# Two transformer blocks on one core: 512-column down products, head sums in parts of the array, refilled gaps and a reworked first stage

## The reference, cut to what matters

```python
x = first_block(x, c, ...)      # 256 tokens, width 2048
#   mod = silu(c) @ w_ada + b_ada -> sh1, sc1, g1, sh2, sc2, g2
#   h = rms_norm(x, mix_norm_pre) * (1 + sc1) + sh1
#   three mixers on h @ w_in, gated and merged, @ w_o
#   x = x + g1 * rms_norm(merged @ w_o, mix_norm_post)
#   h = rms_norm(x, mlp_norm_pre) * (1 + sc2) + sh2
#   y = square(relu(h @ w_up)) @ w_down           # 2048 -> 8192 -> 2048
#   x = x + g2 * rms_norm(y, mlp_norm_post)
return second_block(x, c_2, ctx_2, ...)
#   the same frame; mLSTM and differential attention over 256 tokens of x
#   and 256 of a context; then conv_ffn, 2048 -> 2 * 5632 -> 2048
```

## Time and profile before

| what | us |
|---|---|
| median of 3 runs | 3325.54 (3325.36 to 3334.14) |
| the profiled execution | 3323.51 |
| its span in the trace | 3321.3 |
| TensorE busy with matmuls | 3223.8 (97%) |
| VectorE busy | 2260.6 (68%) |
| ScalarE busy | 1332.6 (40%) |

### The profile page before, as it was taken

How to read it: one execution, slowest core, us unless ns; L and a number is a source line. 1 busy time by engine, 2 the same in 40 slices (tenths; PEclk the granted TensorE clock), 3 DMA queues, 4 the chain that set the end, 5 groups by cost and what they waited for, 6 DMA issues and landing times.

```text
span 3321.3 us, 59467 instructions
## 1 busy us (share of the span) xinstructions
PE 3223.8 (97%) x26148; PEld 3119.3 (94%) x26148; DVE 2260.6 (68%) x2625; ACT 1332.6 (40%) x1455; POOL 1.7 (0%) x10
## 2 busy tenths in 40 slices
PE   7899999999999999999998999999998999999998
PEld 6899999999998999999998898989888999999998
DVE  2499765688876778898856756644756666666664
ACT  2343344434444433333454224422455444343444
POOL 0000000000000000000000000000000000000000
PEclk9999999999999999999999999999999999999999
DMA  9864443488893877777744763354333475655643
GB/s 356 335 209 163 153 153 136 175 330 330 313 347 141 311 286 264 261 253 279 274 164 153 304 239 144 127 211 161 115 139 121 173 253 190 216 209 194 237 165 122
DMA packets 106429, 722.87 MB, mean 218 GB/s; under 512 B 11676, under 2 KB 15388, under 8 KB 27196
## 3 DMA queue, kind: packets, MB, share of 16 engines
q1 hardware_dynamic: 100368, 703.64, 57.4%
q10 hardware_dynamic: 5804, 15.43, 1.5%
HBM read 712.40 MB, written 6.55 MB: 216 GB/s over the span
## 4 chain that ended last, share of the span: by engine, by line
PE 92%; DVE 3%; DMA 2%; ACT 1%; issue 1%; ACTq 0%; DVEq 0%
PE gemm L1006 52%; PE gemm L1015 26%; PE mix L1094 2%; DMA sb_raw<-stream 2%; PE mix L1006 1%; PE mix L1193 1%; PE gemm L1129 1%; PE mix L1457 1%; ACT sb_parts L516 1%; DMA sb_arena<-x_t 1%; DVE sb_arena L1722 1%; DVE sb_parts L1676 1%; PE mix L1015 1%; PE gemm L1530 0%; PE gemm L1523 0%
## 5 line engine op out<-in xcount | busy, mean ns | idle before, releaser
L516 ACT ACTIVATE sb_parts<-sb_raw 128x2048 fp32r<-128x2048 f32 (+2 forms) x499 | 913.7, 1834 | 1668.0 <-PE gemm L1015 1412.3
L1676 DVE TENSOR_TENSOR sb_parts<-sb_raw,sb_parts 128x2048 fp32r<-128x2048 f32 (+2 forms) x499 | 1089.9, 2186 | 401.6 <-ACT sb_parts L516 220.3
L1006 PE MATMUL gemm<-op_h,sb_parts 128*128 128x256 f32 x7232 | 898.5, 282 | 0.5 <-DVE sb_arena L1783 0.5
L1006 PEld LDWEIGHTS gemm<-op_h,sb_parts 128*128 128x128 f32 x7232 | 874.6, 188 | 1.5 <-issue 0.9
L1015 PE MATMUL gemm<-op_h,sb_parts 128*128 128x256 f32 x3616 | 466.3, 282 | 0.0
L1006 PE MATMUL gemm<-op_up,sb_parts 128*128 128x256 f32 x3456 | 438.5, 283 | 11.4 <-DVE op_up L2245 11.4
L1015 PEld LDWEIGHTS gemm<-op_h,sb_parts 128*128 128x128 f32 x3616 | 445.3, 188 | 0.0
L1006 PEld LDWEIGHTS gemm<-op_up,sb_parts 128*128 128x128 f32 x3456 | 422.7, 189 | 13.7 <-DVE op_up L2245 12.2
L1015 PE MATMUL gemm<-op_up,sb_parts 128*128 128x256 f32 x1728 | 228.2, 283 | 0.0
L1657 DVE CUSTOM_DVE_ANT_0 sb_raw<-sb_raw,sb_arena,sb_vec 128x2048 f32<-128x2048 f32 x96 | 224.2, 2348 | 1.1
L1015 PEld LDWEIGHTS gemm<-op_up,sb_parts 128*128 128x128 f32 x1728 | 216.2, 190 | 0.0
(11 more groups left out here) (339 smaller groups left out, 3302.6 us busy)
## 6 DMA issues: line engine op xcount, KB each, us to landing
sb_raw<-stream SPq DMA_DIRECT2D x611, 1024.0 KB, 5.0
sb_raw<-stream SPq DMA_DIRECT2D x64, 704.0 KB, 4.4
sb_raw<-stream SPq DMA_DIRECT2D x16, 768.0 KB, 7.6
sb_arena<-c_rows ACTq DMA_DIRECT2D x3, 1024.0 KB, 8.4
bias_rows<-sb_arena ACTq DMA_DIRECT2D x1, 2304.0 KB
sb_arena<-x_t ACTq DMA_DIRECT2D x4, 512.0 KB, 17.8
sb_arena<-ctx_t SPq DMA_DIRECT2D x1, 2048.0 KB, 10.7
x_keep<-sb_arena ACTq DMA_DIRECT2D x1, 2048.0 KB, 6.2
```

Source lines behind the costliest of these rows:

```text
L516: act.activation(parts[:, b % 2, 0, 0:kt, :], raw[:, slot, 0:kt, :], ACT.Copy).then_inc(hi_ready, 1)
L1006: ins = pe.matmul(out, l, r, start=(opens and i == 0 and x is xh), stop=False, skip_group_check=True)
L1676: dve.tensor_tensor(parts[:, b % 2, 1, 0:kt, :], raw[:, slot, 0:kt, :], parts[:, b % 2, 0, 0:kt, :].bitcast(F32), ALU.subtract).then_inc(t ...
```

## The change

1. `down_round` and `gemm_parts` replace `plain_round` and `gemm_T` in all down sections. The 32 high-weight matmuls of 256 columns become 16 of 512, whose moving operand is high and low half of `op_up` together; the two halves of the bank are added by VectorE (`add_halves`), or, in the first section, copied by ScalarE and added by VectorE (`first_round`).
2. `head_row` puts the 8 sums into four 32-column parts of the array, `spread_rows` spreads from four 32-row parts. VectorE now waits for all four banks at once.
3. In the three gaps the second block's splits move behind the root (ScalarE) and behind `residual` (VectorE). `gemm_two` takes 16 of its 32 low matmuls between the high ones. `norm_x` has 20 small matmuls of ones before it and 10 behind (`keep_warm`). In the middle gap there is no `norm_x`: the second block's `m_k` comes first, and the context's half of its first two blocks is multiplied there, with the norm of x between.
4. First stage: slots grow from 4 to 8 for the first 48 blocks. TensorE handles the shift's A block only; the scale's is stored like the later ones and reduced on VectorE (`scale_column`), by a row of silu(c) made at the start with four matmuls and four activations.

```diff
+            def gemm_parts(b, op, it=0, kt=KT, waits={}):
...
+                for k in range(kt):
...
+                    pe.matmul(out, parts[:, b % 2, 0, k, :], op[:, :, k, :], start=(k == 0), stop=False, skip_group_check=True)
+                pe.wait_ge(taken[slot], uses + 1)
+                for k in range(kt):
+                    ins = pe.matmul(bank(b)[:, 0:S], parts[:, b % 2, 1, k, :], op[:, 0, k, :], start=False, stop=(k == kt - 1),
...
+            def add_halves(acc, b):
+
+                step(dve.tensor_tensor(acc, bank(b)[:, 0:S], acc, ALU.add))
+                dve.tensor_tensor(acc, bank(b)[:, S:512], acc, ALU.add).then_inc(bank_read[BANK[b]], 1)
```

```diff
+                return pe.matmul(M[0][32 * g:32 * g + 32, 0:S], head_sum[:, 31 - j:63 - j], src, start=(j == 0), stop=(j == 1))
...
+                for j in range(2):
+                    for g in range(4):
+                        q = slice(32 * g, 32 * g + 32)
+                        ins = pe.matmul(M[g][:, j * S:(j + 1) * S], ident[q, 32 * g + j:32 * g + j + 1].to_broadcast([32, P]), rows[q, :],
...
+            def keep_warm(n):
...
+                for _ in range(n):
+                    pe.matmul(M[3][:, 0:P], ones[:, :], ones[:, :], start=True, stop=True)
...
+                        if k < KT // 2:
+                            with_low(i, k)
```

```diff
+EARLY_SLOTS, N_EARLY = 8, 48
...
-    + [("m_q", "G" * 8), ("m_k", "GAA" * 8), ("m_g", "G"), ("m_v", "GAA" * 8), ("m_o", "G" * 8),
+    + [("m_k", "GG" + "GAA" * 6), ("m_q", "GGA" * 4), ("m_g", "G"), ("m_v", "GAA" * 8), ("m_o", "G" * 8),
...
+                else:
+                    for c in range(4):
+                        context_part(1, range(4 * c, 4 * c + 4), 0, (0, 1))
+                        norm_part(sqx, *CHUNKS[c + 1])
...
+            def scale_column(r):
...
+                dve.wait_ge(loaded[slot], 16 * (uses + 1))
+                dve.tensor_tensor_reduce(w, w, c1_early, 1.0, v("b_ada", KT + r), ALU.mult, ALU.add, mod1[:, KT + r:KT + r + 1])\
+                   .then_inc(taken[slot], 1)
+                dve.wait_ge(taken[slot], uses + 1)
```

More of the change, by code:

```diff
@@ L763, in _ @@
                     silu_c(cctx_row, 3)
-                    rounds("down1_0", plain_round("down1_0", down1))
+                    rounds("down1_0", first_round("down1_0", down1))
                 elif q < 3:
@@ L968, in _ @@
                 if q == 0:
-                    rounds("down2_0", plain_round("down2_0", down2))
+                    rounds("down2_0", first_round("down2_0", down2))
                 elif q < 3:
@@ L1035, in features_wide, with gemm_two, with_low @@
                 product(b, [(out, True, [(lambda w, x, k=k: (w[:, k, :], x), opW[:, :, 0, k, :], opW[:, :, 1, k, :]) for k in range(KT)])])
-            def gemm_two(b, op, n):
+            def gemm_two(b, op, n, at=0):
+                def with_low(i, k):
+                    return pe.matmul(bank(b + i)[:, at:at + S], parts[:, (b + i) % 2, 1, k, :], op[:, 0, k, :], start=False,
+                                     stop=(k == KT - 1), skip_group_check=True)
                 for i in range(2):
+                    slot, uses = use(G_AT[b + i])
                     pe.wait_ge(hi_ready, b + i + 1)
+                    pe.wait_ge(taken[slot], uses + 1)
                     if NTH[b + i] > 0:
@@ L1110, in ada @@
                     g = k % 4
[L1111 to L1112 removed]
+                    ins = pe.matmul(rows[32 * g:32 * g + 32, 0:P], cpad[:, k, 32:64], slot_of(slot)[:, k, :],
+                                    start=(k < 4), stop=(k >= KT - 4), skip_group_check=True)
                 ins.then_inc(taken[slot], 1)
@@ L1153, in _ @@
             pe.wait_ge(fills, 4)
+            pe.wait_ge(c_one_in, 16)
+            for n in range(4):
+                ins = pe.matmul(G[n][:, :], ones[0:1, :], c1_early[0:1, n * 512:(n + 1) * 512], start=True, stop=True)
+            ins.then_inc(c_spread, 1)
             pe.wait_ge(c_ready, 1)
@@ L1157, in _ @@
                 if r < KT:
-                    for j in range(2):
-                        ada(2 * r + j, j)
+                    ada(2 * r)
                 if r == 3:
@@ L1238, in _ @@
                 if s in (36, 37):
-                    for h in range(6) if s == 36 else range(6, 8):
+                    for h in (0, 2, 4, 1, 3, 5) if s == 36 else (6, 7):
                         pe.wait_ge(o_sq, h // 2 + 1)
-                        ins = pe.matmul(M[0][0:8, 0:S], head_sum[:, 7 - h:15 - h], fP[:, h, :], start=(h == 0), stop=(h == 7))
+                        ins = head_row(h, fP[:, h, :])
                     if s == 37:
@@ L1270, in _ @@
             pe.wait_ge(rstd_ready, norms[0])
-            for h in range(8):
-                ins = pe.matmul(M[h // 2][:, (h % 2) * S:(h % 2 + 1) * S], ident[0:8, h:h + 1].to_broadcast([8, P]), rstd[0:8, 0:S],
-                                start=True, stop=True)
-                if h % 2 == 1:
-                    ins.then_inc(heads_mm, 1)
+            spread_rows(rstd[:, 0:S])
             gate_chunk(2)
@@ L1580, in _ @@
                     pe.wait_ge(dexp, 16)
-                    for h in range(6):
+                    for h in (0, 2, 4, 1, 3, 5):
                         norm_of_head(h)
@@ L1588, in _ @@
             pe.wait_ge(rstd_ready, norms[0])
-            rows = dk[0:8, 0, 0:S]
-            for h in range(8):
-                ins = pe.matmul(M[h // 2][:, (h % 2) * S:(h % 2 + 1) * S], ident[0:8, h:h + 1].to_broadcast([8, P]), rows,
-                                start=True, stop=True)
-                if h % 2 == 1:
-                    ins.then_inc(heads_mm, 1)
+            spread_rows(dk[:, 0, 0:S])
             w_out_a_chunk(23)
@@ L1956, in _ @@
             gains(mod1[:, 32:48], v("mix_post", 0, 16), 48)
-            only_split("w_o")
+            for k in range(KT - 1):
+                split_low(gb("w_o", k) + 2)
             ada_made(80)
@@ L1991, in _ @@
                 if q == 0:
-                    only_split("down1_0")
+                    first_round("down1_0", down1, 0)
                 elif q < 3:
@@ L2253, in _ @@
                 if q == 0:
[L2254 removed]
+                    first_round("down2_0", down2, KT)
                 else:
```

195 lines of the change are left out of this document (128 added, 67 removed).

## The result

The changed kernel takes 3220.4 us (median of 4 runs, 3208.3 to 3236.1) where the kernel before takes 3325.5: a ratio of 0.968 (95% interval 0.963 to 0.973). The forecast was 3280, with 3270 to 3296 as its range. The sign was right, and 60 us of gain were missing.

What follows compares the result with a forecast made beforehand. TensorE, busy 97% of the span, was taken to bound the kernel. Terms 8.0 + 8.6 + 11.6 + 8.2 + 9.3 - 0.5 = 45.2 us off 3323.5 gave 3278.3, stated as 3280 with the runs' median 2.0 higher; range 3270 to 3296.

Steps and rivals of the forecast that it cites:

- first term: Down blocks: joining two 256-column matmuls into one of 512 saves 5.0 ns a pair, 8.6 us over 1728 pairs.
- Down products: Down blocks: 1728 pairs made one gain 8.6 us; blocks 5.62 us apart in down1, 3.86 in down2.
- Rival (c): Down blocks: a pair gains only a fixed 2.5 ns, 4.3 us in all, giving 3284; chance 0.09.
- First stage: Opening stage: more slots and less TensorE work per round gain 8 us, bounds 2 and 14.
- a round cannot be shorter than: First stage: VectorE's 5.5 us from turn to split's end, then low matmuls and next turn, limit a round to 7.1 us.
- Rival (a): First stage: transfers are already at their limit, gain 2 in place of 8, giving 3288; chance 0.15.
- Per-head norms: Sums and spreads at both sites: array parts side by side and a held clock gain 11.6 us, bounds 6 to 13.
- rival (b): Per-head norms: array parts don't run side by side, term 3.6 in place of 11.6, giving 3288; chance 0.09.
- Gaps: After w_o 4.8 us and after w_out_b 3.4 us gained, together 8.2; bounds 4 and 9.
- middle gap: Between down1 and the token products: reordered second-block work gains net 9.3 us, bounds 5 to 11.
- Half a microsecond at the end: After the very last down block: VectorE's added half lies open for 0.42 us, counted as a 0.5 us loss.
- Rival (d): Down sections: denser stream lowers TensorE's granted clock; at 0.90 it costs 67 us, giving 3347; chance 0.03.

Runs made afterwards that it cites:

- The run at the place of the kernel before: Changed kernel with its operands back at the addresses of the kernel before, head_sum allocated behind everything else: 3282.5 us (0.986).
- place 192: Moving operands start 192 bytes behind their address in the kernel before, as in the changed kernel (3220.4 us); the kernel before so moved: 3288.3 us (0.988).
- the run with pairs: Changed kernel with operands at the addresses of the kernel before and each 512-column down matmul issued as two of 256: 3289.5 us (0.988).
- place 0: Moving operands at their address in the kernel before; changed kernel there: 3282.5 us (0.986).
- 240: Operands 240 bytes on modulo 256 (16 bytes below): changed kernel 3202.7 us, beside pairs 3203.6; with pairs 3195.8; kernel before 3227.0.
- trial: Two successive blocks in a kernel of matmuls alone over zeros, operand start varied: 113.3 to 120.0 ns at most places for 256 columns.
- place 64: Moving operands 64 bytes behind their address in the kernel before: kernel before 3258.2 us (0.978), changed kernel 3220.8 us (0.967).
- place 128: Moving operands 128 bytes behind their old address, in the kernel of matmuls alone: 120.0 ns for 256 columns, 227.1 to 229.8 for 512.

## Why the forecast was wrong, step by step

The run at the place of the kernel before has every edit of the diff and the old pace, so that its timeline can be laid beside the old one and each term read by itself. Starts that mark the ends of stages, first of the kernel before, then of the changed kernel at that place:

```profile
152.87 4.04 PE L1006 MATMUL gemm<-op_h,sb_parts 128*128 128x256 f32 x32 [0.45 <-DVE sb_arena L1783]
...
551.71 0.93 PE L1290 MATMUL mix<-sb_arena 64*128 64x128 f32 x6
...
1028.51 3.96 PE L1006 MATMUL gemm<-op_h,sb_parts 128*128 128x256 f32 x32
...
1760.37 0.70 PE L1094 MATMUL mix<-sb_arena,sb_ones 128*128 128x256 f32 x2 [0.53 <-ACT sb_arena L484]
...
1927.98 12.26 PE L1006 MATMUL gemm<-sb_parts,op_hw 128*128 128x256 f32 x102
...
2437.89 2.33 PE L1539 MATMUL mix<-sb_arena,sb_head_sum 128*8 128x256 f32 x10
...
2463.14 3.96 PE L1006 MATMUL gemm<-op_yd,sb_parts 128*128 128x256 f32 x32
...
2543.84 3.96 PE L1006 MATMUL gemm<-op_h,sb_parts 128*128 128x256 f32 x32
...
3307.29 0.70 PE L1094 MATMUL mix<-sb_arena,sb_ones 128*128 128x256 f32 x2 [0.53 <-ACT sb_arena L484]
```

```profile
140.63 4.04 PE L1031 MATMUL gemm<-op_h,sb_parts 128*128 128x256 f32 x32 [0.45 <-DVE sb_arena L1895]
...
514.16 1.06 PE L1244 MATMUL mix<-sb_arena,sb_head_sum 128*32 128x256 f32 x12
...
531.72 1.15 PE L1252 MATMUL mix<-sb_rstd,sb_ident 32*128 32x256 f32 x16
...
535.63 0.90 PE L1363 MATMUL mix<-sb_arena 64*128 64x128 f32 x6 [0.69 <-DVE sb_arena L1991]
...
1006.97 4.06 PE L1031 MATMUL gemm<-op_h,sb_parts 128*128 128x256 f32 x32 [0.29 <-ACT sb_parts L530]
...
1734.46 0.70 PE L1143 MATMUL mix<-sb_arena,sb_ones 128*128 128x256 f32 x2 [0.99 <-ACT sb_arena L498]
...
1892.28 7.99 PE L1031 MATMUL gemm<-sb_parts,op_hw 128*128 128x256 f32 x66
...
2403.64 1.06 PE L1244 MATMUL mix<-sb_arena,sb_head_sum 128*32 128x256 f32 x12
...
2410.69 1.14 PE L1252 MATMUL mix<-sb_arena,sb_ident 32*128 32x256 f32 x16
...
2417.36 2.90 PE L1031 MATMUL gemm<-op_yd,sb_parts 128*128 128x256 f32 x15 [3.44 <-ACT sb_arena L951]
...
2424.64 3.96 PE L1031 MATMUL gemm<-op_yd,sb_parts 128*128 128x256 f32 x32
...
2502.53 4.06 PE L1031 MATMUL gemm<-op_h,sb_parts 128*128 128x256 f32 x32 [0.29 <-ACT sb_parts L530]
...
3267.30 0.70 PE L1143 MATMUL mix<-sb_arena,sb_ones 128*128 128x256 f32 x2 [0.99 <-ACT sb_arena L498]
```

The steps of the difference from mark to mark are what each stage gained (-) or lost (+) (the early sums of the first site before, 525.23, are in the earlier trace rows):

| stage, up to the mark | before | changed, old place | step, us | forecast |
|---|---|---|---|---|
| first stage, to `a_f` | 152.87 | 140.63 | -12.2 | -8 |
| to the early sums | 525.23 | 514.16 | +1.2 | 0 |
| sums and spread of the first site | 551.71 | 535.63 | -5.0 | -4.3 |
| gap after `w_o`, to the first whole `up1` block | 1028.51 | 1006.97 | -5.5 | -4.8 |
| `up1`, `down1` | 1760.37 | 1734.46 | -4.4 | -5.1 |
| middle gap, to the token products | 1927.98 | 1892.28 | -9.8 | -9.3 |
| to the early sums of the second site | 2437.89 | 2403.64 | +1.5 | 0 |
| sums and spread of the second site | 2463.14 | 2424.64 | -4.3 | -7.3 |
| gap after `w_out_b` | 2543.84 | 2502.53 | -2.8 | -3.4 |
| `up2`, `down2`, last norm | 3307.29 | 3267.30 | +1.3 | -3.0 |
| sum | | | -40.0 | -45.2 |

**The step that failed** is none of the listed ones. It is the sentence of the forecast on which its first term rests, and silently all the others: that matmuls keep the pace of their rows, 118.7 and 232.3 ns. At place 192 they have 115.4 and 228.9. Over 19,617 narrow and some 2,500 wide matmuls that is 63 and about 9 us, and the span goes from 3281.3 to 3210.0, 71 us. No rival had this, and the range, made of the bounds of the costed edits, could not hold it. The widened `head_sum` was read as free.

**Down products.** At the old place a down1 block takes 5.62 us and the `down1` sections gain 1.2 us each, 4.6 ns a pair where 5.0 were forecast; the run with pairs agrees with 7.0 us in all, 4.1 ns a pair. But the wide rows of `opW` gave the right price only for their place. Rival (c), a fixed 2.5 ns a pair, falls: 4.6 at place 0, about -7 at 240 ((5.44 - 5.55) / 16). The Trainium skill (TensorE: Matmul & The Clock Gate, Back-to-back issue gap) has warm matmuls N / 2.4 + 2.5 ns apart, and calls that the gap of a single matmul, not of a stream with weight loads. As an estimate by it that is 109.2 and 215.8 ns here. No trial came down to it: the lowest were 113.3 and 226.7. In `down2` the 3.5 us of the forecast didn't arrive: behind the wait for the last `up2` tiles TensorE's granted clock is 0.62 and 0.57 in the first two sections (2622 to 2626.5, 2814 to 2818), where the same stretches of the kernel before had 1.00. The wait is the same 2.3 us.

**First stage.** Direction right, 4 us too small, for two reasons. The transfers didn't stop at the 374 GB/s of `down1_0`, and the chain on VectorE was shorter than the 7.1 us which "a round cannot be shorter than". Two turns, the first low matmul between them and the stretch of the rounds (columns of the last row as in rows 2), in the changed kernel at the old place:

```profile
117.30 0.28 PE L1177 MATMUL mix<-sb_sel,sb_arena 128*128 128x8 f32 x2
...
122.48 0.50 PE L1186 MATMUL gemm<-op_h,sb_parts 128*128 128x256 f32 x2 [0.85 <-DVE sb_parts L1768]
...
124.00 0.29 PE L1177 MATMUL mix<-sb_sel,sb_arena 128*128 128x8 f32 x2
```

```profile
60.00:130.00 70.00, 60.66 (x717) 56.21 (x716) 53.72 (x74) 21.60 (x31) 0.00 (x0) 1.00 1.01 421
```

A round is 6.70 us: 5.18 from `turn` to the split's end where 5.5 was reckoned, and 1.52 behind it. The queue moves 421 GB/s through eight slots, and TensorE waits for VectorE's split, no longer for transfers. Rival (a) falls.

**Per-head norms.** Sums and spreads came as forecast: 1.0 us for six sums (0.9 forecast), 1.1 for each spread (1.0). Parts of the array do run side by side, four row parts into four banks too, and rival (b) falls. At the first site the clock is held and the gain is 0.7 larger. At the second the term was mis-sized by 3 us: behind the faster spread TensorE now waits 3.44 us for the high operand from ScalarE, the clock is 0.60 behind that wait (2417.4 to 2421), and the first block ends 13.95 us after the spread's start where I had reckoned 11. The forecast named that wait's length and not what a wait of such length does to the clock, although show it.

**Gaps.** The sum of 8.2 measured 8.3, and the middle gap's 9.3 measured 9.8. Inside the first two the shares differ: the norm takes 8.5 us, not 7 to 7.5, for it is paced by the squares, and the buffer hand-over costs 0.29, not 0.5. Half a microsecond at the end, for the second addition, is there (the wait 0.53 became 0.99).

**Rival (d)**, a lower clock from the denser stream, didn't happen: the mean granted clock is 0.994 where it was 0.988, and it is 1.00 in the down blocks of the changed kernel (1050 to 1145, 1225 to 1320). The single dips that appear in new spots (0.66 at 431 to 436, where the old kernel had 1.00) are behind waits of 2 us, and are of the size of the +1.2 of the table; the +1.5 was not followed up.

So at equal pace the costed sum is 5 us short in the profiled runs: the first stage gave 4 more, `down2` 4 and the second site 3 less, and the dips took the rest. The medians say 46.8 (3329.3 to 3282.5), since the runs of the kernel before scatter by 10 us. That the old place lands within 2.5 us of the forecast is therefore in part luck: errors of 3 to 4 us in single terms went both ways.

## What to carry to other kernels

An allocation that grows is an edit of every instruction behind it: before a matmul's duration is taken from the old trace, see whether the change moves the addresses of its operands, and if it does, carry "all matmuls 5% faster or 1% slower" as a case of its own. In a kernel bound by TensorE, try the start of the moving operands modulo 256 bytes against that of the weights early: here 16 bytes were worth 101 us to the kernel before, and the whole change 47 at the old place and 24 at the best one. Time an edit at more than one place, since its worth (the wide matmul gained 7 us at one and lost 8 at another) can belong to the place.

## What the hardware did that I had not expected

- The pace of fp32r matmuls with new weights each time depends on the distance between the start of the moving operand and that of the weights, modulo 256 bytes: 113.3 to 120.0 ns for 256 columns, 226.7 to 236.7 for 512, at full clock and with no other engine at work.
- At some distances there are two levels (113.3 and 117.8 at places 64 and 192) and a running stream keeps the one that it entered with. Wide matmuls in it can switch it. What decides at the entry is open. That this is also why the runs of one kernel at places 64 and 192 lie 11 to 28 us apart is a guess: only one run of each kernel was traced, and while the changed kernel at place 0 stays within 5 us, the kernel before, at place 0 too, has up to 18 between its runs.
- The order of places is not the same for narrow and wide matmuls: place 64 has the best narrow pace (113.3 in most trials) and a slow wide one (233.3, where place 128 has 227.1 to 229.8).
- The transfer queue of the first stage moved 421 GB/s where it had 353. Eight slots instead of four came together with less work on TensorE per round; no run separates the two.
